# One ring of four slots for split weights, and the next stage's splits issued ahead of the norm

## The reference, cut to what matters

```
for l in 0, 1:                       # first kind
    mod = silu(c) @ mod_w[l] + mod_b[l]                      # nine vectors of 1024
    x = ln(ALPHA*x + 0.5*(1+g1) * swiglu(x*(1+sc1)+sh1, W1[1024,5632], W2[2816,1024]))
    x = ln(ALPHA*x + (1+g2) * mixer(x*(1+sc2)+sh2))          # l=0: RG-LRU + GLA ("even")
                                                             # l=1: MLA attention ("odd")
    x = ln(ALPHA*x + 0.5*(1+g3) * swiglu(x*(1+sc3)+sh3, ...))
for l in 0, 1:                       # second kind
    h = x + 0.5*swiglu(rms(x)); h = h + window_mixer(rms(h)) # window attention + 31-tap conv, gates, w_o
    h = h + 0.5*swiglu(rms(h)); x = h + (p @ W_proj) * sigmoid(rms(h) @ W_gate)      # "extra"
```

## Time and profile before

| | us |
|---|---|
| median of three timed runs | 2704.56 |
| the profiled execution, its own time | 2708.49 |
| its span | 2706.7 |
| TensorE matmuls busy | 2453.3 (91%) |
| VectorE busy | 1605.9 (59%) |
| ScalarE busy | 1234.3 (46%) |
| GpSimd busy | 171.0 (6%) |
| DMA, mean over the span | 171 GB/s |

### The profile page before, as it was taken

How to read it: one execution, slowest core, us unless ns; L and a number is a source line. 1 busy time by engine, 2 the same in 40 slices (tenths; PEclk the granted TensorE clock), 3 DMA queues, 4 the chain that set the end, 5 groups by cost and what they waited for, 6 DMA issues and landing times.

```text
span 2706.7 us, 44621 instructions
## 1 busy us (share of the span) xinstructions
PE 2453.3 (91%) x18540; PEld 2359.9 (87%) x18540; DVE 1605.9 (59%) x1670; ACT 1234.3 (46%) x1277; POOL 171.0 (6%) x185
## 2 busy tenths in 40 slices
PE   4989889899989886889979999889999999988998
PEld 4989789799989875679979998789999998878998
DVE  5872685485378534265445548855545545975545
ACT  2332655444355333245445446555445535545544
POOL 0110000010001000000001100001100100000110
PEclk9998999899999977789999999999998999999999
DMA  8993333395459722035525543334544554234552
GB/s 328 342 340 120 125 125 138 112 327 214 142 211 340 271 84 94 16 142 200 181 100 183 183 160 121 109 125 178 181 158 149 179 185 156 94 109 145 182 185 97
DMA packets 74218, 462.24 MB, mean 171 GB/s; under 512 B 8515, under 2 KB 8771, under 8 KB 26620
## 3 DMA queue, kind: packets, MB, share of 16 engines
q1 hardware_dynamic: 53136, 383.80, 39.5%
q0 software_dynamic: 18976, 68.71, 6.9%
q10 hardware_dynamic: 1996, 8.12, 0.8%
HBM read 459.53 MB, written 1.06 MB: 170 GB/s over the span
## 4 chain that ended last, share of the span: by engine, by line
PE 70%; DVE 18%; ACT 8%; issue 3%; DMA 1%; ACTq 0%; DVEq 0%
PE ab L1501 38%; PE acc L1501 22%; DVE wlo L851 5%; ACT whi L378 3%; DVE sc L1329 3%; PE mb L1649 2%; DVE sc L934 2%; PE mb L1615 2%; PE mb L1774 1%; DMA par<-params 1%; ACT sc L503 1%; PE mb L1578 1%; DVE u_lo L997 1%; DMA modmem<-mods 0%; DVE sc L1232 0%
## 5 line engine op out<-in xcount | busy, mean ns | idle before, releaser
L851 DVE TENSOR_TENSOR wlo<-raw,whi 128x2048 fp32r<-128x2048 f32 x361 | 826.4, 2290 | 654.9 <-ACT whi L378 654.8
L378 ACT ACTIVATE whi<-raw 128x2048 fp32r<-128x2048 f32 x361 | 690.8, 1914 | 1036.6 <-PE ab L1501 552.2
L1501 PE MATMUL ab<-u_hi,whi 128*128 128x256 f32 x3664 | 1062.8, 290 | 91.2 <-DVE u_lo L997 70.7
L1501 PE MATMUL ab<-u_lo,whi 128*128 128x256 f32 x3664 | 1050.3, 287 | 0.0
L1501 PE MATMUL ab<-u_hi,wlo 128*128 128x256 f32 x3664 | 1049.4, 286 | 0.0
L1501 PEld LDWEIGHTS ab<-u_hi,whi 128*128 128x128 f32 x3664 | 716.8, 196 | 112.4 <-issue 92.3
L1501 PEld LDWEIGHTS ab<-u_lo,whi 128*128 128x128 f32 x3664 | 717.9, 196 | 0.4
L1501 PEld LDWEIGHTS ab<-u_hi,wlo 128*128 128x128 f32 x3664 | 717.2, 196 | 0.0
L1501 PE MATMUL acc<-h_hi,whi 128*128 (+1 forms) x1760 | 512.5, 291 | 24.7 <-DVE wlo L851 17.6
L1501 PE MATMUL acc<-h_lo,whi 128*128 (+1 forms) x1760 | 506.2, 288 | 0.0
L1501 PE MATMUL acc<-h_hi,wlo 128*128 (+1 forms) x1760 | 505.8, 287 | 0.0
(11 more groups left out here) (288 smaller groups left out, 2025.3 us busy)
## 6 DMA issues: line engine op xcount, KB each, us to landing
raw<-stream SPq DMA_DIRECT2D x365, 1024.0 KB, 4.8
modmem<-mods POOLq DMA_DIRECT2D x128, 512.0 KB, 6.0
sc<-start ACTq DMA_DIRECT2D x4, 1024.0 KB, 16.7
modmem<-toep POOLq DMA_DIRECT2D x8, 192.0 KB, 6.8
x<-xT ACTq DMA_DIRECT2D x1, 1024.0 KB, 31.6
sc<-wbd ACTq DMA_DIRECT2D x1, 1024.0 KB, 5.1
outT<-x SPq DMA_DIRECT2D x4, 256.0 KB, 2.5
par<-params ACTq DMA_DIRECT2D x1, 661.5 KB, 26.6
```

The costliest lines, as they stand in the source:

```text
L378: nc.scalar.activation(whi[:, n % SPLIT, :], raw[:, n % RAW, :], ACT.Copy).then_inc(hi_ready, 1)
L851: nc.vector.tensor_tensor(wlo[:, n % SPLIT, :], raw[:, n % RAW, :], whi[:, n % SPLIT, :].bitcast(F32), ALU.subtract).then_inc(lo_ready, 1)
L1501: ins = nc.tensor.matmul(out, l, r, start=first and i == 0, stop=last and i == 2, skip_group_check=True)
```

## The change

`wlo` becomes a second name for the memory of `raw`: the subtraction writes its result over the raw block. `whi` gets four slots instead of two, so the memory in use is the same. A block's slot is now n mod 4 everywhere, from its load to its last matmul. SP therefore waits for `blk_done` of block n-4 and no longer for its low split, and `split_hi` has no wait for `blk_done` of its own (a loaded block implies it). In B stages every block issues a split; `catch_up` and its calls are gone, so two splits of the next stage are in the queues of ScalarE and VectorE ahead of the norm. SPLIT is renamed AHEAD, value 2. `...` marks what is left out; the rest of the diff is that renaming and `% SPLIT` to `% RAW` in the matmul functions.

```diff
-SPLIT = 2
+AHEAD = 2
+RING_AT = 16512
...
         raw = sb("raw", [P, RAW, BLK])
-        whi = sb("whi", [P, SPLIT, BLK], F32R)
-        wlo = sb("wlo", [P, SPLIT, BLK], F32R)
+        wlo = nc.alloc_sbuf_tensor_at("wlo", [P, RAW, BLK], F32R, offset=RING_AT)
+        whi = sb("whi", [P, RAW, BLK], F32R)
...
-            with sp.Fori(0, NBLK // RAW - 1) as it:
+            for g in range(RAW, RAW + START):
+                sp.wait_ge(lo_ready, g - RAW + 1)
+                sp.dma_start(raw[:, g % RAW, :], stream[g]).then_inc(raw_ready[g % RAW], 16)
+
+            with sp.Fori(0, NBLK // RAW - 2) as it:
                 for j in range(RAW):
-
-                    sp.wait_ge(lo_ready, at(j + 1, it))
-                    sp.dma_start(raw[:, j, :], stream[bass.ds(at(RAW + j, it), 1)].rearrange("a p n -> p (a n)"))\
+                    sp.wait_ge(blk_done, at(j + 1, it))
+                    sp.dma_start(raw[:, j, :], stream[bass.ds(at(2 * RAW + j, it), 1)].rearrange("a p n -> p (a n)"))\
                         .then_inc(raw_ready[j], 16)
             for g in range(NBLK // RAW * RAW, NBLK):
-                sp.wait_ge(lo_ready, g - RAW + 1)
+                sp.wait_ge(blk_done, g - START - RAW + 1)
...
                 act.wait_ge(raw_ready[n % RAW], at(16 * (n // RAW + 1), it, 16))
-                if n - START >= SPLIT:
-                    act.wait_ge(blk_done, at(n - START - SPLIT + 1, it))
-                nc.scalar.activation(whi[:, n % SPLIT, :], raw[:, n % RAW, :], ACT.Copy).then_inc(hi_ready, 1)
+                nc.scalar.activation(whi[:, n % RAW, :], raw[:, n % RAW, :], ACT.Copy).then_inc(hi_ready, 1)
...
             def b_blocks(n):
 
                 for i in range(n):
-                    if i < n - 1:
-                        split_hi(g[0] + SPLIT)
+                    split_hi(g[0] + AHEAD)
                     g[0] += 1
                 ph[0] += 1
-
-            def catch_up():
-                split_hi(g[0] - 1 + SPLIT)
...
-                for j in range(8, FFN_B - 1):
-                    split_lo(g[0] + j + SPLIT)
+                for j in range(8, FFN_B):
+                    split_lo(g[0] + j + AHEAD)
...
-                catch_up()
                 inv_std()
```

More of the change, by code:

```diff
@@ L426, in ffn @@
                     for j in range(RAW):
-                        split_hi(g[0] + j + SPLIT, it)
-                for j in range(8, FFN_B - 1):
-                    split_hi(g[0] + j + SPLIT)
+                        split_hi(g[0] + j + AHEAD, it)
+                for j in range(8, FFN_B):
+                    split_hi(g[0] + j + AHEAD)
                 g[0] += FFN_B
@@ L510, in norm2 @@
                 cnt["x"] += 4
-                if (l, which) != (0, 0):
-                    catch_up()
                 for q in range(4):
@@ L850, in split_lo @@
                 dve.wait_ge(hi_ready, at(n - START + 1, it))
-                nc.vector.tensor_tensor(wlo[:, n % SPLIT, :], raw[:, n % RAW, :],
-                                        whi[:, n % SPLIT, :].bitcast(F32), ALU.subtract).then_inc(lo_ready, 1)
+                nc.vector.tensor_tensor(wlo[:, n % RAW, :], raw[:, n % RAW, :],
+                                        whi[:, n % RAW, :].bitcast(F32), ALU.subtract).then_inc(lo_ready, 1)
             def done(n, it=None):
@@ L857, in pass_by @@
             def pass_by():
-                split_lo(g[0] + SPLIT)
+                split_lo(g[0] + AHEAD)
                 g[0] += 1
@@ L886, in ffn_pair @@
                 b = (a[0] + 2 * k) % 2
-                split_lo(n + 2 * k + SPLIT, it)
+                split_lo(n + 2 * k + AHEAD, it)
                 done(n + 2 * k + 1, it)
@@ L971, in ffn @@
                     for j in range(RAW):
-                        split_lo(g[0] + j + SPLIT, it)
-                for j in range(8, FFN_B - 1):
-                    split_lo(g[0] + j + SPLIT)
+                        split_lo(g[0] + j + AHEAD, it)
+                for j in range(8, FFN_B):
+                    split_lo(g[0] + j + AHEAD)
                 g[0] += FFN_B
@@ L1044, in norm2 @@
                 u_lo_pairs(3)
-                if scale is not None:
-                    catch_up()
                 cnt["std"] += 1
@@ L1586, in b_block @@
                 split_ready(n, it)
[L1587 to L1588 removed]
+                wh = whi[:, n % RAW, :].rearrange("p (k c) -> p k c", k=2)
+                wl = wlo[:, n % RAW, :].rearrange("p (k c) -> p k c", k=2)
                 for m in range(DM):
```

49 lines of the change are left out of this document (20 added, 29 removed).

## The result

The changed kernel takes 2659.59 us (three runs, 2657.61 to 2661.50) against 2704.56: ratio 0.9834, 95% interval [0.9815, 0.9854], 45.0 us less. Its profiled execution took 2661.5 us, its span went from 2706.7 to 2659.7 (-47.0). The forecast was 2666 with a span shift of -38.4. The profiled execution of the kernel before (2708.49) is slower than any of its timed ones here or in the experiments (the longest took 2706.5), so shifts against its trace come out 2 to 5 us larger than the medians say.

What follows compares the result with a forecast made beforehand. TensorE's matmuls bound most of the kernel; some 60 of 2706.7 us were within reach. 15.8 + 11.2 + 2.5 + 6.4 - 2.5 + 5.0 = 38.4 us gave 2666 us, own range 2660 to 2673, 80% range 2657 to 2688.

Steps and rivals of the forecast that it cites:

- part 1: Vector loops of four FFNs: without the high split's wait, iterations fall from 24.45 to 23.36 us; 15.8 us gained.
- 3a: Norms after FFNs 0, 1, 2: next stage's splits finish before the last block, TensorE's 3.62 us wait shrinks; 11.2 us gained.
- 3c: Norms after even and odd mixer and six RMS norms: x update 0.8 us earlier at each; 6.4 us gained.
- 3e: Window mixers' B stages: block 5 split before the combine step, net 2.5 us earlier, twice; 5.0 us gained.
- 3d: First extra stage: the next stage's second split comes on top and delays the x update; 2.5 us lost.
- Rival A: DMA binds in the vector loops, iterations stay at 24.2 to 24.45 us; total about -24, 2680 us; 15%.
- Part 2: Reloads wait for the finished block, subtraction in place: loads have 4.5 us to spare; 0, bounds -4 to +4 us.
- rival E: Mean matmuls and first blocks run cheaper after shorter waits; 45 us or more gained, 2657 us; 8%.
- 3b: Norm after FFN 3, which has only one vector: gate ready at 1375.2, y stood at 1377.66; 2.5 us gained.
- the A stages' waits on low splits: Sign in the vector loops: TensorE's wait on low splits (29 places) goes down to about 15.
- the missing waits for the residual sum after FFNs 0 to 2: Sign in these norms: TensorE's 3.6 us waits for the residual sum L1009 fall to 0.3.
- w_o's unbroken blocks: Sign in the window mixers: w_o's second block runs right behind its first.

Runs made afterwards that it cites:

- E4: E1 with the high split's wait for the end of block n-2 kept: 2708.72 us, ratio 1.0021.
- E3: Only a quarter of each vector piece behind the first four loaded: changed kernel 2646.43 us (0.9797), kernel before 2695.80 us (0.9970).
- the second execution: The changed kernel run and profiled again, unaltered: 2658.95 us, ratio 0.9834.
- E5: E1, but in the window mixers w_o's second block is split ahead of the combine step: 2633.68 us, ratio 0.9745.
- E1: The changed kernel's ring of four slots with the order of before (last B block issues no split, catch_up inside the norm): 2637.94 us, ratio 0.9763.
- E7: The kernel before, with the last eight vector blocks of the first and third FFN spread behind the first eight B splits: 2679.45 us, ratio 0.9923.

## Why the forecast came out right, step by step

Time and sign were right, and 2659.6 is 6.4 under the forecast, inside the range and 0.4 under the forecast's own one. But the sum came out by errors of opposite sign: part 1 gave 6.1 us less than forecast, 3a 8.8 more, 3c and 3e together 6.0 more, 3d 1.1 more. The terms as found add up to 48.2 of the span's 47.0. That the errors left so little over is luck.

- **Part 1**: forecast -15.8, found -9.7 (block starts in the chain of waits: -3.5, -3.7, -1.7 and -0.8 in the four FFNs). The loops did what was said: up to the static vector blocks they gained 4.7, 3.7, 5.9 and 0.8, together 15.1 of the forecast 15.3, and E4 shows that the wait alone set their 24.45. The failed term is the one after the loop, where I counted 0.5 us of gain: the stretch from the first static vector block to B block 2 grew from 15.3 to 16.5 us in the first FFN and from 15.9 to 20.1 in the third, and VectorE's waits for vector loads from 5.7 to 17.2. The loop's higher rate isn't what did it, since E4 has the same growth with the loop at 24.45; what E4 shares with the changed kernel is the ring with its later reload. Rival A placed this in the iterations; it is real only behind them (E3).
- **Part 2**: forecast 0 (-4 to +4). This is the step behind the last one: the sum put a later reload at nothing because a weight load had 4.5 us to spare and "GpSimd's vector loads keep their own condition". In the loops the weight loads did have that room, and TensorE did not come to wait for them: 23.31 us is its own time. But in E4 the vector loads that share the DMA with them land later where eight of them are wanted in a row, 4.2 and 4.1 us in the two FFNs. E4's timed runs say +2.7 to +8.4 in all.
- **Part 3a**: forecast -11.2, found -5.0, -7.1, -7.9, together -20.0. The wait went as described (3.62 to none). The size was off by TensorE's clock: I took 0.4 us per norm for it from one mean matmul group of the first norm, while after the second FFN the mean matmuls gave 0.99, the second half of the last block 0.87 and the variance sum 1.69. I gave that 8% as rival E; it is not an alternative but an addition. The variance sum's part (1.69 in two of the three norms, 3.4 in all) is not shown to come from the missing wait, since E4 has it with the wait in place.
- **3b**: forecast -2.5, found -2.5.
- **3c**: forecast -0.8 each, found -0.9, -2.0, -1.0 and -2.0 at the RMS norms behind FFNs, -2.6 after the even mixer and -0.4 after the odd. The update did move by the landing of N1's load, as worked out; the larger ones have cheaper first blocks.
- **3d**: forecast +2.5, found +1.4.
- **3e**: forecast -5.0, found -2.7 and -3.6 between landmarks, and 1.4 and 0.8 already gained in the stages ahead of them (0.5 and 0.8 in the second execution). TensorE's wait behind the conv norm grew from 3.05 to 4.86, +1.8 for +1.7. E5 puts the early split of block 5 at 0.4 and 1.8, far from the 2.5 behind it.

Of the signs that the prediction named, the iterations (23.31), the A stages' waits on low splits (17 for "about 15"), the missing waits for the residual sum after FFNs 0 to 2 and w_o's unbroken blocks came; the DMA share came out at 0.91 and not near 0.98.

What I never asked is what order would be best once the wait is gone. 3c compared with before and found 0.8 us; against the ring with the old order the same step loses. E1 is the comparison that 3c needed.

The bandwidth reasoning was wrong in one number. I had extrapolated 346 GB/s at share 0.95 to 364 at 1.0, but the changed kernel moves 378 GB/s over 29 us at 0.96 and 363 over an iteration at 0.91. The Trainium skill (DMA: Bandwidth & Descriptors, Bandwidth, "Where 436 GB/s comes from") gives about 358 GB/s per core for the HBM side. Both stretches are above it, so here the measurement decides, and their waits are not explained by that figure. The same page of the Trainium skill (Bandwidth, Measured) describes it as what each core gets when both cores of an HBM domain stream. Only one core runs here, so by that page it was no bound for this kernel to begin with.

## What to carry to other kernels

When a change consists of a resource and an order that the resource allows, run the resource with the old order too: here the ring was worth 64 us by the medians (67 by the spans) and the new order took 21 of them back. And when a change moves transfers in time, ask what other transfers they will then stand beside: the ring's later reload was free for the weights and, as far as E4 shows, cost 4 us in each of two places that wait for vector loads. A split issued ahead of a norm is only free if its load has landed; look at what stands first in the in-order queue when a chain begins, and ask of each such item whether anybody needs it before the next thing in the queue. The largest single find, eight vector blocks ahead of a split (26 us), stood in the wait list of before as two waits of 7.4 and 7.9 us that I had left as they were.

## What the runs showed of the hardware

- The same 16 variance matmuls take 5.41 us at granted clock 0.68 and 3.72 at 1.00, and which of the two they get did not follow from the last block's wait. In the kernel before they took 3.72 after FFN 0 behind a wait of 3.62, and 5.41 after FFN 1 behind one of 3.59; in E4, with the same waits, 3.7 in all six norms; the changed kernel took 5.41 after FFN 3 in one execution and 3.72 in the other. What decides it no run here shows. Shifts of 1.7 us between two traces can be this and nothing else.
- Four mean matmuls behind a wait of 3.6 us took 1.13 to 2.08 us (before, E4, E7), without a wait 1.02 or 1.13.
- A DMA share of 0.95 did not mean that DMA was the limit: at 0.61 the iteration took the same 24.45 us. Nor does the rate at one share extrapolate: 346 GB/s at 0.95, 352 at 0.88 (E4), 363 at 0.91 and 378 at 0.96.
